# Expert rows gathered from the spilled rows and scaled after the gather; the seventh down slot filled in the output projection

## The reference

```python
h = modulate(rms_norm_2(x, norm2_g[l]), shift2, scale2)
# route: group softmax and argmax over 4 groups, top 2 of the group's 8 experts
dest = p_starts[se] + jnp.arange(n_assign) - starts[se]      # place of each (token, choice)
xg = ht[slot_tok].reshape(n_blocks, MOE_BLOCK, D)            # rows gathered by expert
a = jax.nn.silu(xb @ w_gate[e]) * (xb @ w_up[e])
out = (a @ w_down[e]) * wb[:, None]
y = zeros.at[slot_tok].add(out)                              # summed back by token
x = x + gate2 * y                                            # then the final norm
```

## Time and profile before

| | |
|---|---|
| Three runs, median (lowest, highest) | 1628.16 us (1625.53, 1631.08) |
| The profiled execution's own time | 1629.59 us |
| Its span, first to last instruction | 1627.6 us |
| TensorE (PE) busy | 1513.5 us, 93% |
| VectorE, ScalarE, POOL busy | 769.8, 454.7, 579.5 us |
| DMA | 260.91 MB, mean 160 GB/s |
| Granted TensorE clock, mean | 0.978 |
| Stage from the output projection on | about 1257 us to the end |

### The profile page before, as it was taken

One profiled execution on the slowest core, in us unless ns is written; L12 is line 12 of the kernel. 1 busy time (PEld: TensorE's weight loads), 2 busy tenths in 40 slices (PEclk: granted clock), 3 DMA queues, 4 the chain that ended last, 5 costly groups with the idle time before them and its releaser, 6 DMA issues.

```text
span 1627.6 us, 21255 instructions
## 1 busy us (share of the span) xinstructions
PE 1513.5 (93%) x8362; PEld 1197.1 (74%) x8362; DVE 769.8 (47%) x1470; ACT 454.7 (28%) x722; POOL 579.5 (36%) x473
## 2 busy tenths in 40 slices
PE   6989999999999999989999999999999989977785
PEld 5978887778888888857888888775688866544442
DVE  2474656378686863237314712345313254432234
ACT  4352334243231323243323241342213121000001
POOL 2571220434454545534443145420154313322122
PEclk9998999999999999989999999999999999999998
DMA  4241110235445442212322122210043699999995
GB/s 167 99 177 51 52 53 1 95 114 207 181 179 207 156 181 92 97 76 103 110 78 78 53 78 90 101 53 27 27 181 129 261 346 360 379 388 371 390 414 209
DMA packets 37347, 260.91 MB, mean 160 GB/s; under 512 B 7280, under 2 KB 7920, under 8 KB 13184
## 3 DMA queue, kind: packets, MB, share of 16 engines
q1 hardware_dynamic: 31488, 251.13, 40.8%
q0 software_dynamic: 5760, 8.41, 1.6%
HBM read 252.69 MB, written 17.30 MB: 166 GB/s over the span
## 4 chain that ended last, share of the span: by engine, by line
PE 84%; DVE 7%; issue 4%; ACT 3%; DMA 1%; POOL 0%; DVEq 0%; SPq 0%; ACTq 0%; POOLq 0%
PE G L2122 13%; PE G L2123 13%; PE G L2124 13%; PE SA L2688 4%; PE G L2688 4%; PE SA L2122 3%; PE SA L2124 3%; PE SA L2123 3%; PE PB L2122 3%; PE PB L2124 3%; PE PB L2123 3%; PE G L2164 2%; PE OB L2312 2%; PE SA L2568 1%; PE OB L2474 1%
## 5 line engine op out<-in xcount | busy, mean ns | idle before, releaser
L760 POOL TENSOR_TENSOR wl<-raw,wh 128x512 fp32r<-128x512 f32 x356 | 479.4, 1378 | 693.2 <-ACT wh L893 688.4
L893 ACT ACTIVATE wh<-raw 128x2048 fp32r<-128x2048 f32 x90 | 172.3, 1914 | 292.6 <-PE SA L2124 152.5
L2122 PE MATMUL G<-Hh,wh 128*128 128x512 f32 x544 | 217.5, 400 | 1.5 <-DVE arena L1547 1.4
L2124 PE MATMUL G<-Hh,wl 128*128 128x512 f32 x544 | 213.5, 392 | 0.0
L2123 PE MATMUL G<-Hl,wh 128*128 128x512 f32 x544 | 213.4, 392 | 0.0
L1618 DVE SCALAR_TENSOR_TENSOR arena<-arena,st 128x256 f32<-128x256 f32 x144 | 132.9, 923 | 5.1
L2124 PEld LDWEIGHTS G<-Hh,wl 128*128 128x128 f32 x544 | 103.0, 189 | 22.4
L2122 PEld LDWEIGHTS G<-Hh,wh 128*128 128x128 f32 x544 | 103.2, 190 | 22.0 <-issue 1.9
L2123 PEld LDWEIGHTS G<-Hl,wh 128*128 128x128 f32 x544 | 103.3, 190 | 19.6
L833 POOL DMA_INDIRECT raw<-xn_rows,arena x38 | 36.6, 964 | 130.2 <-PE G L2704 106.5
L2122 PE MATMUL G<-wh,Hh 128*128 128x256 f32 x256 | 76.7, 300 | 0.0
(11 more groups left out here) (528 smaller groups left out, 3107.3 us busy)
## 6 DMA issues: line engine op xcount, KB each, us to landing
raw<-in_pieces_dram SPq DMA_DIRECT2D x91, 1024.0 KB, 4.8
arena<-in_pieces_dram SPq DMA_DIRECT2D x24, 1024.0 KB, 4.8
arena<-in_wexp_dram SPq DMA_DIRECT2D x11, 2048.0 KB, 37.9
dn_w<-in_wexp_dram SPq DMA_DIRECT2D x18, 1024.0 KB, 40.8
arena<-in_wexp_dram SPq DMA_DIRECT2D x12, 1024.0 KB, 28.1
gu_y<-in_wexp_dram SPq DMA_DIRECT2D x6, 2048.0 KB, 32.7
gu_z<-in_wexp_dram SPq DMA_DIRECT2D x5, 2048.0 KB, 43.7
gu_h<-in_wexp_dram SPq DMA_DIRECT2D x4, 2048.0 KB, 37.6
```

The source lines that it names most:

```text
L760: ins = pool.tensor_tensor(low_[:, part], whole[:, part], high[:, part], ALU.subtract)
L893: act.activation(split_pair(s)[0], wait_raw(act, sp_list[s]), ACT.Copy).then_inc(S("high_split"), 1)
L2122: pe.matmul(out, ah, bh, start=first, stop=False)
L2124: return pe.matmul(out, al, bh, start=False, stop=last)
```

## The change

The rows are gathered from the spilled X itself, whose tensor now has the layout of 512 rows by 1024; both spills and both reads back use it. The gathered rows are not yet divided by their root mean square. ScalarE multiplies each gathered block in place by a column of roots before TensorE transposes it. The column comes from a second product with the 0/1 matrices, in which the entry of a pair is the root of its token. The copy of normed rows and its store are gone, and the squares go to the first half of `raw`. So the second half of `raw` is free once the last piece is split, and down 6 is issued right behind down 3. Gate/up 6 is issued when the spill has landed. In the overflow blocks POOL copies a third small column, and ScalarE scales after tanh. Several semaphores for roots become one, `heads_rstd`.

```diff
-        x_spill = nc.dram_tensor("x_spill", (P, NT * D), F32).ap()
+        x_spill = nc.dram_tensor("x_spill", (T, D), F32).ap()
+        x_spill_tiles = x_spill.rearrange("(t p) n -> p t n", p=P)
...
-        xn_rows = nc.dram_tensor("xn_rows", (T, D), F32).ap()
-        xn = raw[:, :].rearrange("p (t n) -> p t n", t=NT)
+        sq_act, sq_vec = raw[:, 0:D], raw[:, D:2 * D].unsqueeze(1).to_broadcast([P, NT, D])
+        slot_one = AR(13824, 8 * (NBLK + 2)).rearrange("p (c n) -> p c n", c=8)
+        slot_rstd = AR(14336, 8 * (NBLK + 2)).rearrange("p (c n) -> p c n", c=8)
+        row_rstd = AT(NBLK + AHEAD)
+        over_rstd = AT(WS)
@@ SP
             expert_dn(2)
             expert_dn(3)
+            sp.wait_ge(S("low_split"), len(split_pieces()))
+            expert_dn(6)
             wait_group(sp, "wout", 7)
             expert_gu(4)
             wait_freed(sp, "wout", 7)
-            sp.dma_start(x_spill, X[:, :]).then_inc(S("x_spilled"), 16)
-            sp.wait_ge(S("rows_normed"), 3 * NT)
-            sp.dma_start(xn_rows.rearrange("(t p) n -> p t n", p=P), xn).then_inc(S("xn_stored"), 16)
+            sp.dma_start(x_spill_tiles, Xv).then_inc(S("x_spilled"), 16)
             expert_dn(4)
             expert_dn(5)
             wait_group(sp, "gr", 0)
             expert_gu(5)
-            for v in range(2):
-                sp.wait_ge(S(f"xg_loaded{v}"), 16)
-            expert_dn(6)
             sp.wait_ge(S("x_spilled"), 32)
             expert_gu(6)
@@ POOL
             pool.wait_ge(S("slot_idx_ready"), 1)
-            pool.wait_ge(S("xn_stored"), 16)
+            pool.wait_ge(S("x_spilled"), 32)
...
+                        pool.tensor_copy(over_rstd[:, v:v + 1], row_rstd[:, bass.ds(b + AHEAD, 1)]).then_inc(S("idx_ready"), 1)
@@ ScalarE
             for t in range(2):
-                act.activation(xn[:, t, :], Xv[:, t, :], ACT.Square, accum_out=ss2[:, t:t + 1])
+                own(act.activation(sq_act, Xv[:, t, :], ACT.Square, accum_out=ss2[:, t:t + 1]))
...
-            act.wait_ge(S("rstd_x"), 5)
-            for t in range(NT):
-                act.activation(xn[:, t, :], Xv[:, t, :], ACT.Copy, scale=rstd2[:, t:t + 1]).then_inc(S("rows_normed"), 1)
...
+            def rows_scaled(b, v, scale):
+                act.activation(xg(v), xg(v), ACT.Copy, scale=scale).then_inc(S("xg_scaled"), 1)
+            act.wait_ge(S("places_ready"), 3)
+            for b in range(2):
+                act.wait_ge(S(f"xg_loaded{b}"), 16)
+                rows_scaled(b, b, row_rstd[half_rows(b), b:b + 1])
             for b in range(NE):
+                v = (b + 2) % AHEAD
+                act.wait_ge(S(f"xg_loaded{v}"), xg_count(b + 2))
+                rows_scaled(b + 2, v, row_rstd[half_rows(v), b + 2:b + 3])
                 if b >= 1:
                     turned_copy(b - 1)
...
                         act.activation(tanhg[:, u, :], GU[u][0:BS, 0:256], ACT.Tanh, scale=0.5).then_inc(S("tanh_ready"), 1)
+                        n = (v + 2) % WS
+                        act.wait_ge(S(f"xg_loaded{n}"), xg_count(NE) + 16 * i + 16 * ((v + 2) // WS))
+                        rows_scaled(b + 2, n, over_rstd[half_rows(n), n:n + 1])
@@ VectorE
+            for k in range(2):
+                ins = dve.tensor_tensor(slot_rstd[:, 4 * k:4 * k + 4, :], slot_one[:, 4 * k:4 * k + 4, :],
+                                        rstd2.unsqueeze(2).to_broadcast([P, NT, NBLK + 2]), ALU.mult)
+            ins.then_inc(S("places_ready"), 1)
...
+            dve.wait_ge(S("slots_rooted"), 1)
+            own(dve.tensor_copy(row_rstd[:, 0:NBLK + 2], SA[1][:, 0:NBLK + 2]))
+            dve.tensor_copy(over_rstd, row_rstd[:, NE:NE + WS]).then_inc(S("places_ready"), 1)
@@ TensorE
+            pe.wait_ge(S("places_ready"), 2)
+            for c in range(8):
+                for u in range(2):
+                    ins = pe.matmul(SA[1][BS * u:BS * u + BS, 0:NBLK + 2], place[:, c, :], slot_rstd[:, c, :], start=c == 0, stop=c == 7)
+            ins.then_inc(S("slots_rooted"), 1)
...
-                pe.wait_ge(S(f"xg_loaded{b % AHEAD}"), xg_count(b))
+                pe.wait_ge(S("xg_scaled"), b + 1)
...
-                        pe.wait_ge(S(f"xg_loaded{(v + 2) % WS}"), xg_count(NE) + 16 * i + 16 * ((v + 2) // WS))
+                        pe.wait_ge(S("xg_scaled"), b + 3)
```

More of the change, by code:

```diff
@@ L673, in _ @@
                     sp.wait_ge(S("values_summed"), A0 + len(aunits))
-                    sp.dma_start(X[:, :], x_spill).then_inc(S("x_back"), 16)
+                    sp.dma_start(Xv, x_spill_tiles).then_inc(S("x_back"), 16)
                 if p == ("cmp", 1, 1):
@@ L777, in _ @@
             pool.wait_ge(S("ss_k"), 1)
-            rstd_of(rqk[:, 0:16], msqk[:, 0:16], ssqk[:, 0:16], 16, HD).then_inc(S("rstd_k"), 1)
+            rstd_of(rqk[:, 0:16], msqk[:, 0:16], ssqk[:, 0:16], 16, HD).then_inc(S("heads_rstd"), 1)
             low(sp_list[6])
@@ L792, in _ @@
             pool.wait_ge(S("ss_attn"), 1)
-            rstd_of(rqk[:, 0:4], msqk[:, 0:4], ssqk[:, 0:4], NT, 512).then_inc(S("rstd_attn"), 1)
+            rstd_of(rqk[:, 0:4], msqk[:, 0:4], ssqk[:, 0:4], NT, 512).then_inc(S("heads_rstd"), 1)
             low(sp_list[16])
             wait_freed(pool, "csq", 0)
-            rstd_of(rqk[:, 4:8], msqk[:, 4:8], ssqk[:, 4:8], NT, 512).then_inc(S("rstd_conv"), 1)
+            rstd_of(rqk[:, 4:8], msqk[:, 4:8], ssqk[:, 4:8], NT, 512).then_inc(S("heads_rstd"), 1)
             for p in sp_list[17:20]:
@@ L820, in _ @@
             own(pool.tensor_scalar(msc[:, 4:8], ssc[:, 4:8], 1.0 / CKV, EPS, ALU.mult, ALU.add))
-            pool.tensor_tensor(rsc, msc, mhalf.to_broadcast([P, 8]), ALU.pow).then_inc(S("rstd_c"), 1)
+            pool.tensor_tensor(rsc, msc, mhalf.to_broadcast([P, 8]), ALU.pow).then_inc(S("heads_rstd"), 1)
             for p in sp_list[NC3 + 3:]:
@@ L850, in _ @@
                     scatter((b - 3) % 2, pair_i[:, b - 3:b - 2])
+            pool.wait_ge(S("places_ready"), 3)
             pool.wait_ge(S("bexp_ready"), 1)
@@ L1357, in _ @@
             low(5)
-            dve.wait_ge(S("rstd_k"), 1)
+            dve.wait_ge(S("heads_rstd"), 1)
             for u in range(2):
@@ L1404, in queries_normed @@
             def queries_normed(j):
-                dve.wait_ge(S("rstd_q"), j + 1)
+                dve.wait_ge(S("heads_rstd"), j + 2)
                 for u in range(2):
@@ L1459, in cmp_step @@
                 if t == 3:
-                    dve.wait_ge(S("rstd_kc"), 1)
+                    dve.wait_ge(S("heads_rstd"), 4)
                     for u in range(2):
@@ L1576, in _ @@
                                          ALU.mult, ALU.subtract).then_inc(S("conv_low"), 1)
-            dve.wait_ge(S("rstd_attn"), 1)
+            dve.wait_ge(S("heads_rstd"), 5)
             for half in range(2):
@@ L1587, in _ @@
                     free_group(dve.tensor_copy(ssqk[:, 4:8], b[:, 0:4]), "csq", 0)
-                    dve.wait_ge(S("rstd_conv"), 1)
+                    dve.wait_ge(S("heads_rstd"), 6)
                 for t in range(NT):
@@ L1787, in _ @@
                 if i == 3:
-                    dve.wait_ge(S("rstd_c"), 1)
+                    dve.wait_ge(S("heads_rstd"), 7)
                     for t in range(NT):
@@ L1909, in _ @@
                     routing_tables()
-            square_last(xn, ss2, "wout", 7)
+            square_last(sq_vec, ss2, "wout", 7)
             for n in (5, 7):
@@ L1984, in _ @@
             iota_b = cols(tab3, TAB3, "iota_b").unsqueeze(1).to_broadcast([P, 8, NBLK + 2])
-            own(dve.tensor_tensor(block_tok, iota_b, dst_b.unsqueeze(2).to_broadcast([P, 8, NBLK + 2]), ALU.is_equal))
-            own(dve.tensor_tensor(block_tok, block_tok, second.unsqueeze(2).to_broadcast([P, 8, NBLK + 2]), ALU.mult))
+            own(dve.tensor_tensor(slot_one, iota_b, dst_b.unsqueeze(2).to_broadcast([P, 8, NBLK + 2]), ALU.is_equal))
+            own(dve.tensor_tensor(block_tok, slot_one, second.unsqueeze(2).to_broadcast([P, 8, NBLK + 2]), ALU.mult))
             dve.tensor_tensor(place, cols(tab3, TAB3, "iota_r").unsqueeze(1).to_broadcast([P, 8, BS]),
                               dst_r.unsqueeze(2).to_broadcast([P, 8, BS]), ALU.is_equal).then_inc(S("places_ready"), 1)
+            for k in range(2):
+                ins = dve.tensor_tensor(slot_rstd[:, 4 * k:4 * k + 4, :], slot_one[:, 4 * k:4 * k + 4, :],
+                                        rstd2.unsqueeze(2).to_broadcast([P, NT, NBLK + 2]), ALU.mult)
+            ins.then_inc(S("places_ready"), 1)
             b = wait_group(dve, "slots", 0)
```

12 lines of the change are left out of this document (6 added, 6 removed).

## The result

The changed kernel took 1632.88 us, median of 20 runs (1630.86 to 1635.05), against 1630.53 for all 20 runs of the kernel before, timed beside it. The ratio is 1.0016, 95% interval 1.0009 to 1.0023: slower by 2.6 us, with 1.5 to 3.7 in the interval. (The ratio leaves out two disturbed runs of the kernel before, of 5754 and 7528 us.) The forecast was +2.0 us, no difference by its bound of 0.3%. The profiled execution's span is 1630.8 us, 3.2 longer than before.

What follows compares the result with a forecast made beforehand. The expert weight stream, released by block 0 freeing its slot, and what follows its last piece bound the kernel. Terms: 0.0 at the stream's start plus 2.0 in the overflow blocks, on a median of 1628.16, gave 1630.2 us; range 1622 to 1637.

Steps and rivals of the forecast that it cites:

- What bounds: Expert stage: the end is set by when the weight stream starts for good and what follows its last piece.
- (a): Before the experts: dropping the normed-row copy and its 2.10 MB store, and gathers waiting for the spill, change nothing: 0.
- rival A: Weight stream from 1302 to 1590: removed bytes count in full, 9.1 us off, giving 1621.1 us; chance 0.13.
- (b): Before block 0: down 6 and gate/up 6 fill early, prefetch completes about 1329.5, first gather 0; cancels with (c).
- the backlog: Before the change, 3.38 MB (down 6, gate/up 6, two gathers) moved ahead of gate/up 7's data, which began at 1342.9.
- the hole of 0.7: DMA idle for 0.7 us after gate/up 7's data, until down 7's data begin at 1349.1.
- (c): Start of block 0: scaling ahead of the first transposes makes gate/up 0 start 1.5 us later, bounds +0.1 to +2.3.
- (d): After the slot products: 16 root matmuls, VectorE products and small copies are covered by existing waits: 0.
- (e): Main loop: each block gains 1.06 us of ScalarE scaling, hidden because gathers are asked for early: 0.
- (f): Two overflow blocks: scaling after tanh delays the activations 1.0 us each, +2.0 us at the diagonals, bounds 0 to +2.3.
- Rival B: Start of experts: TensorE runs at its lower clock, the stream starts 7 us late, giving 1637.2 us; chance 0.13.
- point of decision: Start of experts: Rival B decides once the low-clock stretch outlasts the holding matmuls by more than 3 us.

Runs made afterwards that it cites:

- e3: Changed kernel plus an unread 2.10 MB copy within device memory, issued when block 0's rows are transposed, while DMA engines idle; ratio 1.0023.
- e4: Changed kernel plus the same unread 2.10 MB copy, issued behind gate/up 13 in the full weight stream; ratio 1.0037.
- e2: Changed kernel with the early fill undone: down 6 and gate/up 6 issued after the first two gathers, as before; ratio 1.0018.
- e12: The changed kernel run once more, unedited; ratio 1.0012.
- e7: Changed kernel with ScalarE scaling only 16 of 1024 columns of each gathered block, part of the computation left out; ratio 0.9995.
- e10: e8 with down 6 and gate/up 6 issued only after the first two gathers; ratio 1.0003, 3.9 us slower than e8.
- e11: e8 with down 6 still early but gate/up 6 issued after the first two gathers have landed; ratio 0.9978.
- e1: Changed kernel with the overflow blocks' scaling moved ahead of the wait for the gate/up product and of tanh; ratio 1.0006.
- e8: Changed kernel with the edits of e1, e5 and e6 together; 1627.23 us against 1630.77, ratio 0.9979.
- e9: Kernel before the change with only the holding-matmul edits of e5 and e6; ratio 0.9993.
- e5: Changed kernel without the three holding matmuls between the transposes of block 1 and gate/up 0; ratio 1.0010.
- e6: Changed kernel with nine instead of five holding matmuls ahead of the first transposes; ratio 0.9994.

## Why the prediction was right

**What bounds.** Shown. Over the seven kernels whose slots were full in time and that have no extra copy, the stream after the release is 230.65 to 231.65 us, while the release itself moved from 36.11 to 39.98. A later release is a later end of the stream, one for one; this is the base of the whole sum.

**(a) and rival A, the removed bytes.** Right: they lengthen the idle stretch only. e3 puts 2.10 MB back there at 0.8 us of stream, e4 puts them into the stream at 3.2. Rival A asked for 9 us less.

**(b) The early fill.** The reckoning of the backlog held in sign: before, the stream had 3.2 us more after its release (234.58 for 231.40). In the changed kernel this repays the late start, and the medians of e2 and the changed kernel are equal within 0.4 us. What I missed is in "the first gather meets the same queue as before: 0": true against before (4.3 us from POOL to the first transposes then, 4.2 to the scaling now), yet the queue costs 1.1 us against an empty one.

The size was not right: by the forecast's own terms the stream was to gain 1.5 us, 2.2 of backlog less the hole of 0.7. About as much as the other 1.7 shows in the rate at which the engines moved bytes, at nearly the same share (columns as in the earlier trace rows; before, then after):

```profile
1345.00:1363.00 18.00, 17.89 (x150) 11.64 (x148) 8.48 (x15) 1.69 (x6) 5.92 (x6) 1.00 1.01 359
1363.00:1383.00 20.00, 19.94 (x162) 11.57 (x161) 9.66 (x18) 2.35 (x8) 6.83 (x7) 1.00 1.01 355
```

```profile
1344.61:1362.61 18.00, 17.89 (x150) 11.45 (x148) 8.73 (x16) 5.40 (x9) 4.91 (x5) 1.00 0.98 385
1362.61:1382.61 20.00, 19.97 (x170) 12.12 (x166) 8.47 (x15) 5.29 (x9) 6.92 (x7) 1.00 1.02 367
```

That is 0.7 MB more in 38 us, some 1.8 us of stream. From 42 to 60 us after the spill the kernels with gate/up 6 issued late moved 341 to 373 GB/s and those with it issued early 377 to 389. Why is not known.

**(c) The late start.** Mis-sized: +1.5 us was the term for gate/up 0, and +2.0 came; the release is 2.6 later. The first scaling began 28.88 us after the spill, where the forecast's landing (1331.94) is 28.94 after it. A scaling of 64 rows took 1.13 to 1.15 us and not 1.06. The rest is mainly clock: gate/up 0 took 4.46 us for 3.91, and the second eight transposes ran at the lower level (sixteen took 2.15 us for 1.21, with the wait for the second scaling in it). The upper bound of this term should read +2.2, two scalings of 1.06 and 0.1; it changes nothing. The Trainium skill (ScalarE: Activation LUTs, What ACT_TABLE_LOAD costs) gives, for 128 partitions, 186 ns plus 0.833 per element of a row, and 93 ns more for a scale that is a column of values. As an estimate from these figures a scaling of 1024 columns takes 1.13 us, and the trace agrees at 64 partitions: 1.13 to 1.15.

With the release 2.6 us late and 3.2 taken off the stream, gate/up 31 came 0.6 us sooner than before (270.92 for 271.52; e12 270.77). The forecast was 0.0. Two errors met here, and that is luck: a release 1.1 us too early in the sum, and a gain of the stream 1.7 us too small.

**(d) and (e).** Right. The root products ran at 1325.62, right behind the slot products, POOL's first gather began 24.7 us after the spill as before, and the hold ended at 1330.11, before the rows came. TensorE never waited for a scaled row in the main loop, and e7's stream is that of the others.

**(f) The tail.** The mechanism is right, 1.7 us of order by e3, e10 and e11 for the 2.0 forecast. The size is not: the tail grew by 4.7, and by 4.1 to 5.0 in five of the other six kernels that scale after tanh. The excess is time at the 1.2 GHz level: 3.0 us here, some 1.6 in e1, e8 and e9 (tails of 30.9 to 31.0), none in e10 and e11. Those five have no stop in front of the row transposes, and e1, e8, e10 and e11 have the same code in their overflow blocks, so a single execution's tail moves by 1.6 us without any edit there. It also means that the 4.7 is in part the luck of the profile of the kernel before: against e9, which has its tail and a stretch of low clock (30.99), the changed kernel's is 3.0 longer. The stretch behind the diagonals was 0.5 us shorter (23.25 for 23.78); over all profiles it is 23.1 to 24.2, so this is no effect of the change.

**Rival B**, the low clock at the start, was partly true: the low stretch outlasted the hold by 1.6 us and not by 3, so it cost about 1 us and not 7. Its point of decision was not reached, so no run tests it. Not every stop brought the lower level: after the stops of 0.90 us and less in e8 and e10 the clock stayed at 2.4 GHz. It matters more than its chance said, since e8 shows what is gained where it does not come.

**The sum**: -0.6 (stream) + 4.7 (tail) - 0.5 (behind) = +3.6 in the profile, less 0.4 for an earlier stage, the 3.2 of the span; +2.6 in the medians. With e9's tail in place of the one before it would be -0.6 + 3.0 = +2.4, near the medians; this is an estimate from two single executions. The forecast of +2.0 had the right two places, 0 at the start and a loss in the tail. That it is so near rests in part on luck, as the start's two errors cancelled, and the clock was left out of the tail.

## What to carry to other kernels

Before counting bytes that a change removes, find what releases the next transfer: with a fixed number of slots, moving less before that release is worth nothing, and filling earlier is worth only what would still be in the queue at it: nothing that could be told with a late start (e2), 3.9 us with an early one (e10 against e8). Then look at the first consumer's latency, for there one microsecond is one microsecond of the end. An operation put on a gathered row belongs ahead of the wait for the product, not behind it, also in the rarely run copy of the loop.

## What the runs showed of the hardware

- TensorE's granted clock fell to the 1.2 GHz level after stops of 1.3 to 3.1 us before the first transposes. After 2.58 to 3.07 us (the changed kernel, e12, e1, e3, e4, e5) the transposes themselves ran at it, in e12 in part; after 2.11 (before), 1.80 (e7), 1.48 (e2) and 1.30 with 0.33 between the two sets (e6) they ran at full clock or nearly, and the holding matmuls behind them were slow. With stops of 0.90 us and less in front of them (e8, e9, e10, e11) all of it ran at 2.4 GHz.
- A copy of 2.10 MB within device memory cost 3.2 us of the weights' stream, less than the 5.5 that these bytes take at the stream's own 384 GB/s.
- A gather of 64 rows behind a draining queue of weights reached ScalarE 4.2 to 4.7 us after POOL began, and 3.1 to 3.2 us with the queue empty (e2, e10, e11).
